# Results of an expert pair ordered by token tile: the down product in 32-column tiles, the scatter on 64 rows and by halves of columns

## What is computed

```python
h = jax.nn.silu(xe @ w1[e]) * (xe @ w3[e])
y = (h @ w2[e]) * g[:, None].astype(xe.dtype)
return out.at[tok].add(y), None
```

## Time and profile before

| | us |
|---|---|
| median of three runs | 1365.6 (1365.51 to 1366.85) |
| profiled execution, own time | 1367.23 |
| its span in the trace | 1365.2 |
| TensorE busy | 1332.6 (98% of the span) |
| VectorE busy | 477.5 (35%) |
| ScalarE busy | 353.9 (26%) |
| GpSimd busy | 85.0 (6%) |

### The profile page before, as it was taken

How to read it: one execution, slowest core, us unless ns; L and a number is a source line. 1 busy time by engine, 2 the same in 40 slices (tenths; PEclk the granted TensorE clock), 3 DMA queues, 4 the chain that set the end, 5 groups by cost and what they waited for, 6 DMA issues and landing times.

```text
span 1365.2 us, 21079 instructions
## 1 busy us (share of the span) xinstructions
PE 1332.6 (98%) x8658; PEld 810.0 (59%) x8658; DVE 477.5 (35%) x795; ACT 353.9 (26%) x874; POOL 85.0 (6%) x99
## 2 busy tenths in 40 slices
PE   8999999999999999999999999999999999999998
PEld 4555676656656555555497557665665655555543
DVE  1584633232332322333501146232332323233344
ACT  1244432232222222222210224323222232222212
POOL 2443100000000000000100021000000000000000
PEclk9999999999999999999999999999999999999999
DMA  9820669999999999999654426699999999999991
GB/s 293 309 96 31 252 244 418 421 421 421 421 421 421 421 421 421 421 420 391 228 202 169 193 83 265 256 421 421 420 421 421 421 421 421 421 421 421 421 362 62
DMA packets 80501, 461.85 MB, mean 338 GB/s; under 512 B 6560, under 2 KB 6784, under 8 KB 31008
## 3 DMA queue, kind: packets, MB, share of 16 engines
q1 hardware_dynamic: 77824, 452.06, 81.8%
q0 software_dynamic: 2592, 8.53, 2.0%
HBM read 459.52 MB, written 1.05 MB: 337 GB/s over the span
## 4 chain that ended last, share of the span: by engine, by line
PE 76%; DMA 16%; DVE 6%; issue 1%; ACT 1%; DVEq 0%; SPq 0%; POOL 0%
PE ps L1153 27%; DMA ring<-in_exp_w_dram 15%; PE ps L1181 12%; PE ps L1199 8%; PE ps L827 4%; PE ps L1312 4%; PE ps L1006 3%; PE ps L931 3%; DVE o_tok L2005 3%; PE ps L1078 2%; PE ps L1030 2%; PE ps L1109 2%; PE ps L1070 1%; PE ps L991 1%; PE ps L847 1%
## 5 line engine op out<-in xcount | busy, mean ns | idle before, releaser
L1181 PE MATMUL ps<-ring,qkT 128*64 128x512 f32 x1024 | 233.8, 598 | 0.0
L2005 DVE TENSOR_TENSOR o_tok<-ps,o_tok 128x1024 f32<-128x1024 f32 x124 | 151.9, 1225 | 81.2 <-PE ps L1199 80.9
L2011 DVE TENSOR_TENSOR y_lo<-ps,y_hi 128x1024 fp32r<-128x1024 f32 x62 | 75.9, 1225 | 217.9 <-ACT y_hi L1547 217.9
L1181 PEld LDWEIGHTS ps<-ring,qkT 128*64 128x64 f32 x1024 | 68.0, 136 | 132.3 <-issue 132.0
L1995 DVE SCALAR_TENSOR_TENSOR roped<-roped,rows,ps 128x256 f32<-128x256 f32 x64 | 30.8, 481 | 316.7 <-ACT roped L1519 316.7
L1153 PE MATMUL ps<-ring,xT 128*64 128x256 f32 x1024 | 122.0, 380 | 7.2 <-DMA ring<-in_exp_w_dram 7.1
L1519 ACT ACTIVATE roped<-ps 128x256 f32<-128x256 f32 x64 | 24.6, 384 | 402.3 <-PE ps L1153 402.3
L1153 PE MATMUL ps<-ring,pT 128*64 128x256 f32 x992 | 122.1, 380 | 1.0 <-DMA ring<-in_exp_w_dram 1.0
L1153 PE MATMUL ps<-ring,proj 128*64 128x256 f32 x1024 | 121.4, 379 | 0.0
L1153 PE MATMUL ps<-ring,gb_row 128*64 128x256 f32 x992 | 121.4, 379 | 0.0
L1199 PE MATMUL ps<-y_hi,selT 128*128 128x512 f32 x248 | 110.5, 446 | 3.0
(11 more groups left out here) (294 smaller groups left out, 1538.5 us busy)
## 6 DMA issues: line engine op xcount, KB each, us to landing
ring<-in_exp_w_dram SPq DMA_DIRECT2D x174, 2048.0 KB, 21.3
ring<-in_exp_w_dram SPq DMA_DIRECT2D x28, 1024.0 KB, 6.8
ring<-in_od_w_in_dram SPq DMA_DIRECT2D x6, 2048.0 KB, 8.3
ring<-in_ple_w_gate_dram SPq DMA_DIRECT2D x4, 2048.0 KB, 15.9
ring<-in_ev_w_in_dram SPq DMA_DIRECT2D x3, 2048.0 KB, 20.4
ring<-in_ev_w_o_dram SPq DMA_DIRECT2D x2, 2048.0 KB, 11.3
ring<-in_exp_w_dram SPq DMA_DIRECT2D x8, 512.0 KB, 17.5
ring<-in_od_w_o_dram SPq DMA_DIRECT2D x2, 2048.0 KB, 7.8
```

The lines of the kernel that those rows point to most:

```text
L1181: ins = pe.matmul(ps[b * SLOTS:(b + 1) * SLOTS, 4 + half, :], hT[:, f, b * SLOTS:(b + 1) * SLOTS], views[b][:, f, half * PIECE:(half + 1) ...
L2005: dve.tensor_tensor(y_acc[:, t, :], ps[:, bank:bank + 2, :].rearrange("p b n -> p (b n)"), y_acc[:, t, :], ALU.add)\
L2011: dve.tensor_tensor(y_lo[:, :], ps[:, 4:6, :].rearrange("p b n -> p (b n)"), y_hi[:, :], ALU.subtract)\
```

## The change

1. `sel_bf` is laid out by pair, tile, expert and slot, so the 128 columns of a pair are filled by both tiles, in the order tile, expert, slot (t, b, s). There are no zeros to clear, and the clearing on GpSimd and VectorE's wait for it go away. One transpose gives `selT`, whose rows 0 to 63 belong to token tile 0 and rows 64 to 127 to token tile 1. The gates come from four matmuls of three columns in tiles of 32 columns.
2. ScalarE copies 128 instead of 256 columns of `selT`, and makes the gates with one instruction instead of two.
3. `exp_down` uses tiles of 32 columns, one for each tile and expert: 16 matmul instructions a pair instead of 8, each with the same 512 moving columns. Its output rows stand in the order (t, b, s).
4. `scatter(m, half)` handles one half of the columns for both token tiles, each tile on its own 64 rows. It is four matmuls of 512 columns, two on each half of the rows. Over a pair it is still eight matmuls.
5. The first half of the scatter moves into `exp_up`, between the two up products. The second half stays ahead of `exp_down`. In the last four pairs both halves stand behind `exp_up`, the second in banks 0 and 1.
6. VectorE adds by halves of columns, with the first add ahead of `gate_h`.

```diff
-                    for t in range(NT):
-                        pe.transpose(ps[:, bank, t * HD:(t + 1) * HD].bitcast(BF16), sel_bf[:, t, own], ident_bf)
-                    for t in range(NT):
-                        cols = slice(2 * m, 2 * m + 2) if isinstance(m, int) else bass.ds(2 * m, 2)
-                        ins = pe.matmul(ps[:, bank, SEQ:SEQ + 6], sel_bf[:, t, own], gates_bf[:, t, :, cols],
-                                        start=(t == 0), stop=(t == NT - 1))
+                    pe.transpose(ps[:, bank, 0:HD].bitcast(BF16), sel_bf[:, u, :, :], ident_bf)
+                    for b in range(2):
+                        for t in range(NT):
+                            q = (b * NT + t) * TILE_SLOTS
+                            ins = pe.matmul(ps[q:q + TILE_SLOTS, bank, SEQ:SEQ + 3], sel_bf[:, u, t, b * TILE_SLOTS:(b + 1) * TILE_SLOTS],
+                                            gates_bf[:, t, :, 2 * m + b], start=True, stop=True)
...
                     for w in range(2):
+                        if w == 1 and scatter_half:
+                            scatter(m - 1, 0, 1 - par)
...
-                                ins = pe.matmul(ps[b * SLOTS:(b + 1) * SLOTS, 4 + half, :],
-                                                hT[:, f, b * SLOTS:(b + 1) * SLOTS],
-                                                views[b][:, f, half * PIECE:(half + 1) * PIECE], start=(f == 0), stop=(f == 1))
+                                for t in range(NT):
+                                    q = (t * 2 + b) * TILE_SLOTS
+                                    h0 = (b * NT + t) * TILE_SLOTS
+                                    ins = pe.matmul(ps[q:q + TILE_SLOTS, 4 + half, :], hT[:, f, h0:h0 + TILE_SLOTS],
+                                                    views[b][:, f, half * PIECE:(half + 1) * PIECE], start=(f == 0), stop=(f == 1))
...
-                    for half in range(2):
-                        for part in (y_hi, y_lo):
-                            ins = pe.matmul(ps[:, bank + half, :], selT[:, par, t * P:(t + 1) * P],
-                                            part[:, half * PIECE:(half + 1) * PIECE],
+                    for part in (y_hi, y_lo):
+                        for t in range(NT):
+                            ins = pe.matmul(ps[:, bank + t, :], selT[tile_rows(t), par, :],
+                                            part[tile_rows(t), half * PIECE:(half + 1) * PIECE],
                                             start=(part is y_hi), stop=(part is y_lo))
...
-                    if scatter_last:
-                        scatter(m - 1, 0, 1 - par, M0 == 0 and isinstance(m, int) and m == 1)
+                    if scatter_last and not gather_next:
+                        scatter(m - 1, 0, 1 - par)
+                        scatter(m - 1, 1, 1 - par, bank=0)
...
-                    if scatter_last:
-                        scatter(m - 1, 1, 1 - par, False, bank=6 if gather_next else 0)
+                    if scatter_last and gather_next:
+                        scatter(m - 1, 1, 1 - par)
                     exp_down(m, par, first and M0 == 0, by_half=not selT_next)
...
-                    act.activation(selT[:, par, :], ps[:, bank, 0:SEQ // 2].bitcast(BF16), ACT.Copy)
-                    for b in range(2):
-                        rows_b = slice(b * SLOTS, (b + 1) * SLOTS)
-                        ins = act.activation(gate_parts[rows_b], ps[rows_b, bank, SEQ + b:SEQ + 6:2], ACT.Copy,
-                                             accum_out=slot_gate[rows_b, par:par + 1])
-                    ins.then_inc(sem("selT_copied"), 1)
+                    act.activation(selT[:, par, :], ps[:, bank, 0:HD].bitcast(BF16), ACT.Copy)
+                    act.activation(gate_parts, ps[:, bank, SEQ:SEQ + 3], ACT.Copy,
+                                   accum_out=slot_gate[:, par:par + 1]).then_inc(sem("selT_copied"), 1)
...
-                    dve.tensor_tensor(y_acc[:, t, :], ps[:, bank:bank + 2, :].rearrange("p b n -> p (b n)"), y_acc[:, t, :], ALU.add)\
-                       .then_inc(sem("y_added"), 1)
+                    dve.tensor_tensor(ys, ps[:, bank:bank + 2, :], ys, ALU.add).then_inc(sem("y_added"), 1)
```

More of the change, by code:

```diff
@@ L1186, in exp_down, with tile_rows, scatter @@
                     ins.then_inc(sem("exp_down"), 1)
-                def scatter(m, t, par, first, bank=6):
-                    if t == 0:
+                def tile_rows(t):
+                    return slice(t * SLOTS, (t + 1) * SLOTS)
+                def scatter(m, half, par, bank=6):
+                    if half == 0:
                         pe.wait_ge(sem("y_split"), m + (M0 + 1))
                     if bank == 0:
+                        if m == PAIRS - 5:
+                            pe.wait_ge(sem("pT_done"), L + 1)
                         pe.wait_ge(sem("y_added"), 2 * m + 2 * M0)
-                    elif not (first and t == 0):
-                        pe.wait_ge(sem("y_added"), 2 * m + (2 * M0 + t))
-                    for half in range(2):
-                        for part in (y_hi, y_lo):
-                            ins = pe.matmul(ps[:, bank + half, :], selT[:, par, t * P:(t + 1) * P],
-                                            part[:, half * PIECE:(half + 1) * PIECE],
+                    elif m + M0 > 0 or half:
+                        pe.wait_ge(sem("y_added"), 2 * m + (2 * M0 + half))
+                    for part in (y_hi, y_lo):
+                        for t in range(NT):
+                            ins = pe.matmul(ps[:, bank + t, :], selT[tile_rows(t), par, :],
+                                            part[tile_rows(t), half * PIECE:(half + 1) * PIECE],
                                             start=(part is y_hi), stop=(part is y_lo))
@@ L1259, in _ @@
                         pe.wait_ge(sem("y_split"), M0 + PAIRS)
[L1260 to L1263, removed]
+                    for part in (y_hi, y_lo):
+                        for t, bank in ((0, 6), (1, 2)):
+                            ins = pe.matmul(ps[:, bank + half, :], selT[tile_rows(t), 1, :],
+                                            part[tile_rows(t), half * PIECE:(half + 1) * PIECE],
                                             start=(part is y_hi), stop=(part is y_lo))
-                        ins.then_inc(sem("scattered_half") if half == 0 else sem("scattered"), 1)
+                            if part is y_lo:
+                                ins.then_inc(sem("scattered_half") if half == 0 else sem("scattered"), 1)
                 with pe.If(flag > 0):
@@ L1961, in one_hot @@
                         own = (dst[:, t, :].rearrange("p (e s) -> p e s", e=8) if dst is sel else
[L1962 to L1965, removed]
+                               dst[:, :, t, :].rearrange("p u (b s) -> p u b s", b=2))
+                        slots = place[:, t, cols]
+                        count = const[:, C_IOTA + 1:C_IOTA + 1 + TILE_SLOTS]
+                        if dst is sel:
+                            slots = slots.unsqueeze(2).to_broadcast([P, 8, TILE_SLOTS])
+                            count = count.unsqueeze(1).to_broadcast([P, 8, TILE_SLOTS])
+                        else:
+                            slots = slots.rearrange("p (u b) -> p u b", u=4).unsqueeze(3).to_broadcast([P, 4, 2, TILE_SLOTS])
+                            count = count.unsqueeze(1).unsqueeze(1).to_broadcast([P, 4, 2, TILE_SLOTS])
+                        ins = dve.tensor_tensor(own, slots, count, ALU.is_equal)
                     return ins
@@ L2042, in dve_step @@
                 def dve_step(m, o, u, build=True, build_bf=True, add=True, second=6):
+                    if add and second:
+                        add_y(m - 1, 0)
                     if isinstance(m, int) and PAIRS - 8 <= m < PAIRS - 4:
-                        dve.wait_ge(sem("y_added"), 2 * (M0 + m - 1))
+                        dve.wait_ge(sem("y_added"), 2 * (M0 + m - 1) + 1)
                         add_shared(m - (PAIRS - 8))
                     gate_h(m, u % 2)
-                    if add:
+                    if add and not second:
                         add_y(m - 1, 0)
```

23 lines of the change are left out of this document (10 added, 13 removed).

## The result

The changed kernel takes 1368.66 us in the median of 20 runs (1365.56 to 1369.83), the kernel before 1366.09 us in the median of 20 (1365.0 to 1368.24). The medians differ by 2.6 us. The ratio over all these runs is 1.0014, with a 95% interval of 1.0007 to 1.0020, which is 1.9 us longer (1.0 to 2.7). So the loss is clear of the noise, but within the 0.2% that the prediction took for about no change. The forecast was 1366.5 us, 0.9 us over before, with a range of 1363 to 1371.

The account below looks back on a forecast made before the run. The prediction took the continuous weight transfers of the expert stages, not TensorE, as the bound. Its terms +0.8 - 0.2 + 0 + 0.3 gave +0.9 us, from 1365.6 to 1366.5 us, range 1363 to 1371.

Parts of the forecast that it names:

- Something behind the last landing became longer by over 2 us: Failure sign, after a stage's last weight transfer: the prediction fails if work there grows by over 2 us.
- What bounds the kernel: Expert stages: continuous weight transfers set the pace at 15.07 us a pair, so TensorE's saving lies hidden under them.
- Down in four tiles: `exp_down`: 32 records in four column tiles run together and take 3.6 us a pair (bounds 3.5 and 7.2).
- the first rival: `exp_down`: four column tiles do not run together, down takes 7.2 us, about 1538 us in all; chance 0.08.
- The pair on TensorE: Expert stages: TensorE's chain of one pair falls to 13.5 us, 0.7 below now and 1.5 below the transfers.
- changes of tiles: TensorE's chain of a pair: about five more switches of tiling at 0.1 us each, 0.5 us.
- Start of the stream: Pair 0, two `sel_transpose` calls at +0.2 us each: weight transfers start 0.4 us later a layer, +0.8 us in all.
- Behind the last landing of layer 0: Last pair of layer 0, up to the start of down: -0.2 us (bounds -0.5 and +1.0).
- Tail of layer 1: After layer 1's last weight transfer: VectorE waits for `gb_row` anyway, so down starting earlier gives 0.
- Instruction fetch: Down's 2048 added records, 0.11 MB at 421 GB/s in the saturated DMA engines: +0.3 us.
- Small costs at the two ends: Pairs 0 and 31: four tiles overlapping like three, or dearer tile changes, +3.3 us more, 1369.8 us; chance 0.15.
- No lower clock from the new waits: Expert stages: TensorE's added waits are not likely to lower its granted clock, which is 1.00 in the attention stage.

Follow-up runs that it names:

- e7: The changed kernel with each pair's gather done three times in 27 pairs of a layer: 1425.31 us, ratio 1.0433 to the kernel before.
- e8: The kernel before with each pair's gather done three times in 27 pairs of a layer: 1445.70 us, ratio 1.0583 to the kernel before unedited.
- e2: The changed kernel with 192 empty instructions more in TensorE's program of layer 0, mid-stage: 1367.54 us, ratio 1.0003 to the kernel before.
- e3: The kernel before with 65 empty instructions more in TensorE's program of layer 0, mid-stage: 1367.57 us, ratio 1.0008 to it unedited.
- e6: The kernel before with 60 empty instructions more in TensorE's program of layer 0, mid-stage: 1367.07 us, ratio 1.0004 to it unedited.
- e9: The kernel before with 512 empty instructions inside layer 0's overflow code, which is jumped over and never runs: 1374.13 us, ratio 1.0055 to it unedited.
- e1: The changed kernel again, unedited, beside the kernel before on one chip: 1369.45 us, ratio 1.0015 to the kernel before.
- e4: The changed kernel with 256 empty instructions more, one whole block, in layer 0's mid-stage: 1368.23 us, ratio 1.0009 to the kernel before.
- e5: The changed kernel with 8 empty instructions more in TensorE's program of layer 0: 1372.87 us, ratio 1.0048 to the kernel before.
- e11: The kernel before with each pair's gather done twice (one extra gather): 1393.44 us, ratio 1.0198 to the kernel before unedited.
- e12: The changed kernel with 40 empty instructions more in TensorE's program of layer 0: 1368.02 us, ratio 1.0008 to the kernel before.

## Where the prediction held and where it did not, point by point

The time came out in the range, and what bounds the kernel was read rightly. But the sum came near the measured time in part by luck: its largest term (+0.8 us) came to about +0.3, its 0.3 us for instruction fetch came to some 3 us in three profiles, and its list of what would show it wrong has an item that came true. "Something behind the last landing became longer by over 2 us" fits layer 0's tail in the profiled execution, 18.4 us from down to the gate for 14.9 before.

**What bounds the kernel: right.** The change takes 448.0 - 437.9 = 10.1 us of TensorE's work out of each expert stage, 20 us in all, and e7 and e8 show all of it (20.4 us) once TensorE sets the pace. With the transfers in front, the stages are 460.3 and 460.4 us against 460.5 and 459.4. Pair 31's w3 landed in layer 0 within 1 us of the forecast: TensorE starts on it at 633.20 us, 633.92 before, and from the issue of pair 2's w2 that is 441.4 us in both. The gain went under the transfers and came out as waits on `ring`.

**Down in four tiles: right.** 3.57 us, as concluded from the earlier trace rows; the first rival, 7.2 us, is out. The Trainium skill ("TensorE: Matmul & The Clock Gate", section "The mechanism") says that matmuls start in strict order; the reading that each tile would then hold back the next, through the two records of a float32 instruction, is not borne out by the 3.57 us.

**The pair on TensorE: direction right, size off.** 13.8 us instead of 13.5. Down was as forecast, and four other pieces took longer: the half scatters 0.66 us each for 0.58, up 7.2 for 6.9, gather 1.15 for 0.94, the transposes of h 0.36 for 0.24. That is 0.8 us for the 0.5 taken for changes of tiles; that the changes are the cause is argued, and no run tests it. The saving over a stage is 10.1 us, 0.37 a pair of 27, for 0.7 forecast. TensorE is busy for 96% of the stages, not 90%, and the waits on `ring` came to 31.9 us for the 80 forecast. I had multiplied a pair's slack by all pairs, although TensorE does not wait at all from 202 to 322 us and has the shared expert's work in four pairs.

**Start of the stream, +0.4 us a layer: less than half of it.** In layer 0, pair 2's w2 is issued 13.18 us behind the start of pair 0's up, 13.03 before: +0.15 us.

```profile
191.84 0.63 SPq L468 DMA_DIRECT2D ring<-in_exp_w_dram  x1
```

In layer 1 it is 13.17 us for 13.06. The `sel_transpose` inside this stretch takes 0.27 us for 0.17; the one ahead of it 0.28 for 0.25 (0.24 in layer 1). Together that is +0.3 us over both layers for the 0.8 forecast. The profiles' stages (six of the changed kernel with and without padding, four of before) have medians of 460.4 and 460.2 us in layer 0, 460.5 and 459.3 in layer 1. The +1.4 us in sum is of the size of my +0.8 and +0.3 for the fetch, but profiles of one kernel differ by nearly as much (459.1 to 460.1 before in layer 1), and no run takes it apart. Nearly all of it is in layer 1, and there the tail takes it back: stage and tail together have medians of 475.3 us in the changed kernel and 475.1 before.

**Behind the last landing of layer 0, -0.2 us: right as far as the term went.** It covered the stretch from the landing of pair 31's w3 to the start of its down. That is 5.76 us in the changed kernel and 6.05 before, 0.3 us won:

```profile
633.20 1.95 PE L1152 MATMUL ps<-ring,xT 128*64 128x256 f32 x16 [1.25 <-DMA ring<-in_exp_w_dram]
...
638.96 3.64 PE L1183 MATMUL ps<-ring,qkT 128*32 128x512 f32 x32 [0.52 <-issue]
```

```profile
633.92 1.95 PE L1153 MATMUL ps<-ring,xT 128*64 128x256 f32 x16 [1.12 <-DMA ring<-in_exp_w_dram]
...
639.97 3.65 PE L1181 MATMUL ps<-ring,qkT 128*64 128x512 f32 x16
```

What comes behind down had no term. Down to product is 5.73 us for 6.11, 0.4 us won. Product to the gate's matmuls (L1320) is 9.17 us without the standstill (e2) and 8.80 before, 0.4 us given back: TensorE waits 0.54 us for VectorE's layer norm instead of 0.28. So the tail from down to the gate is 14.9 us in both without the standstill. With it, it is 18.4.

**Tail of layer 1, 0: right as to the change.** In the profiled executions it looks 1.3 us shorter (14.9 for 16.2), because the wait on `gb_row` is gone. But of the four profiles of before and its padded forms (before, e3, e6, e9) two show that wait and two do not, at 14.9 us. None of the six of the changed kernel shows it.

**Instruction fetch, +0.3 us: right part, wrong mechanism.** I costed it as bytes in a saturated queue, and the bytes were about right (0.14 MB more for 0.11). Its price is latency behind a branch: 2.4, 3.5 and 2.7 us of standstill in three profiles of three (the changed kernel, e1, e4), and half a clock for 3.4 us behind two of them; the tail up to the gate is 2.8 to 3.7 us longer in these traces. That is the mis-sized term. How much of the +1.9 us it makes over all runs is not settled: with it padded away (e2) the change measures +0.4 us (-0.8 to +1.6), which fits that it makes most, but the intervals of e1 and e2 overlap. "Small costs at the two ends", the rival that came nearest, named the tiles, and it was not they.

**No lower clock from the new waits: not in general.** In one of the six profiles of the changed kernel (e1) the clock fell to half behind a wait of 2.03 us for the weights; in the five others it did not fall in the expert stages.

## What to carry to other kernels

Ask of any saving on an engine whether that engine sets the pace over the whole stage, and test it with a dose: here twenty us of TensorE's work went for nothing, and one extra gather a pair showed how much room there is, better than one pair's rows did. In a program with branches, a change in the number of instructions moves every later piece of code against the blocks in which it is fetched; look for an "issue" wait behind a branch and for a lower clock after it before a small difference is put down to the edit. Longer skipped code can cost time though it never runs (7.5 us in e9). And one trace is one execution: compare its time with the spread of the runs before its standstill is taken for that of all of them.

## What the runs showed of the hardware that was not expected

- Behind TensorE's branch over the overflow code, in both layers of all 14 traces, a block's fetch starts 3.5 to 6.0 us after the branch (3.5 to 3.9 in 17 of the 28 cases). Where TensorE stood, it went on 2.3 to 2.7 us after the start of the fetch that it waited for: 0.9 to 1.1 us of packet time and 1.3 to 1.7 after it.
- The granted clock was at 0.50 for 3.4 us after stands of 2.4 and 2.7 us, for 6.8 us around stands of 1.85, 4.4 and 5.4 us, for 10.2 us around one of 6.7 us, and not at all around one of 3.5 us (e1).
- In e3, e5, e7, e11 and e12 the clock also fell for 3.4 us in the mixer of layer 1 (at 686 to 715 us), which made the stretch from layer 0's gate to layer 1's first up product 203.2 us long instead of 201.6, in either kernel; in e1 it fell at the last pair of layer 0, whose stage was 462.6 us. Falls of this size can make up part of the 4 us over which the runs of one kernel spread.
- A wait that is long met takes 0.11 us of TensorE's queue as an instruction of its own (the padding in e2's trace).
